# Moving operands on a fixed byte phase, forget gates without their own slab, and a shifted order of splits in a three-block transformer kernel

## The chip, the cores and the metric

One core of a Trainium2 chip runs the whole program; the other cores are idle. The metric is the device time of one execution in microseconds (us), median of the runs shown. Engines are named as in the profile: PE (TensorE matmul) with PEld (its weight loads), DVE (VectorE), ACT (ScalarE), POOL (GpSimd), SP (SyncE, which here only issues transfers).

## The reference, cut to what matters

256 tokens (272 with 16 meta tokens in front in the first layer) of width 1024 pass through three layers, all in fp32.

```python
# first_block: a = rmsnorm(h); proj = a @ w_in -> pool mixer, "forgetting" attention, stick-breaking attention
log_f = log_sigmoid(fl + forget_bias)      # fl = a @ w_in[:, 6 columns]: the forget gates, one per head
c = cumsum(log_f); s = q k^T * scale + c[q] - c[k]          # forgetting attention
h = h + concat(y_pool, y_fox, y_sb) @ w_out
h = h + (silu(rmsnorm(h) @ w_gate) * (rmsnorm(h) @ w_up)) @ w_down
# second_block, layer 0: convolution branch + block attention, h @ ab_w_out, then squared-ReLU MLP (4096 wide)
# second_block, layer 1: conv, two block-diagonal gates, linear recurrence, h @ c_w_out, then the same MLP
```

Nearly all arithmetic is in products of the 1024-wide activations with weights that are read once.

## The kernel before

**Slabs.** Every weight matrix is cut into slabs of 128 x 1024 fp32 (512 KB), 275 in all, laid out in the order of use and brought in by SP into a ring of `R` = 4 buffers `raw`. To get fp32 precision from single-pass matmuls each slab is split: ACT writes the rounded high part (`whi`, line 513), DVE subtracts to get the rest (`wlo`, line 929). Activations are split in the same way into `ahi` (ACT, lines 541, 572, 622) and `alo` (DVE, lines 947, 953), and the hidden values of the MLPs into `hidhi` and `hidlo`. A product is then three matmuls: `whi*ahi`, `whi*alo`, `wlo*ahi` (function `three`, lines 1363 to 1365).

**Columns and rows.** A slab is used in one of two forms, 24 matmuls each. As a *column* (`column`) it gives 128 output channels: the weights of chunk k meet the tokens of chunk k of `ahi`/`alo`, for k = 0 to 7, and all 24 add into one PSUM bank. As a *row* (`row`, `operand_row`, `hidden_row`) it takes one chunk of 128 inputs, so all 24 read the same chunk of tokens, and they add into 8 half banks. The MLPs alternate columns (tokens from `ahi`/`alo`) with rows (from `hidhi`/`hidlo`). The output projections OUT1, OUT2 and OUT3 are 8 rows each, row i on chunk i of `ahi`/`alo`; OUT3's first two take their chunk from `hidhi`/`hidlo` instead. Each stage begins with `first_columns`, where two columns are interleaved chunk by chunk while DVE still makes `alo`.

**Stages, with the slabs they use.** IN1 (21: one for the forget gates and 20 columns), OUT1 (8), MLP1 (66: 44 columns, 22 rows), IN2 (20 columns), OUT2 (8), MLP2 (64: 32 and 32), IN3 (16 columns), OUT3 (8), MLP3 (64). IN1's columns that also serve the meta tokens read 272 tokens from a chunk's start; all others read 256 from its 17th.

**Where the tokens lie.** A chunk of `ahi` or `alo` is 272 fp32 = 1088 bytes, that is 4 x 256 + 64. In the built program `ahi` begins at byte 82,560 of each partition and `alo` at 91,264, both 128 past a multiple of 256. Token 16 of chunk k therefore lies at byte (192 + 64 k) mod 256: 192 for k = 0 and 4, 0 for k = 1 and 5, 64 for k = 2 and 6, 128 for k = 3 and 7. `hidhi` begins at 134,720 with 1024-byte chunks, so all its chunks lie at byte 64 of 256, and so do those of `hidlo`. All weight chunks lie at byte 128.

**Forget gates.** The first slab holds the six gate columns, padded with zeros to 128. It is an ordinary column, interleaved with the first real one at the start of the program, where four *pieces* of two chunks each arrive, are split and are used one after the other. Lines 1032 to 1043 on DVE turn its result into the running sum `cum`.

**Constants.** POOL builds masks, the identity and so on from 18 us on; the semaphore `consts` counts them, and `consts_done` = 13 means all. PE waits for all 13 before the value transposes (line 1458) that follow IN1's first columns, and DVE waits for them before the scan at line 1043.

**Order.** No scheduler moves anything. The order on each engine is that of the code, by hand-written tables: `DVE_SPLITS`, `CAT2_STEP`, `RESIDUAL_ROW`, `FINAL_RESIDUAL` say in which slot `u` of the OUT2 stage DVE makes which split, `alo` and residual. `split_ahead(n)` splits slab n + 3.

## Time and profile before

| | |
|---|---|
| median of 3 runs | 887.29 us (886.36 to 1056.22) |
| profiled execution | 886.04 us |
| its span, first to last instruction | 884.3 us |
| PE busy | 868.6 us (98%), 7310 matmul records |
| PEld, DVE, ACT, POOL busy | 837.4, 607.5, 470.6, 95.0 us |
| HBM traffic | 169 GB/s over the span |
| chain that ended last | PE 87%, DVE 7%, ACT 3%, issue 1%, DMA 1% |

The span is the time between the first and the last instruction of the profiled execution; 1.7 us of the device time lie around it. A matmul's own duration in the profile overlaps its neighbours', so what a matmul costs is read from the start of one to the start of the next. An fp32 matmul has two records, one of the split kind has one.

### The profile page before, as it was taken

What the parts mean: (1) busy time and instruction counts of PE and PEld (TensorE: products, weight loads), DVE (VectorE), ACT (ScalarE), POOL (GpSimd) and SP (SyncE); (2) the same over time, 40 slices, a digit from 0 to 9 for tenths busy, and PEclk for the clock granted to TensorE, in tenths of its full rate; (3) what the DMA queues carried; (4) which work ended last, traced back from release to release, by engine and by line L of the source; (5) the groups of instructions that cost most, each with busy time, mean ns of one, the idle gap of its engine ahead of it and who ended that gap; (6) DMA issues with size and microseconds to landing.
All of it is one profiled execution on the core that took longest, in us unless ns stands there. A gap on an engine that the chain in (4) does not pass through costs nothing.

```text
span 884.3 us, 19363 instructions
## 1 busy us (share of the span) xinstructions
PE 868.6 (98%) x7310; PEld 837.4 (95%) x7310; DVE 607.5 (69%) x994; ACT 470.6 (53%) x755; POOL 95.0 (11%) x139
## 2 busy tenths in 40 slices
PE   8999999999999999999999999999999999999996
PEld 8888899999999999787999999999999999999996
DVE  4766558666566587877866666668979966666665
ACT  6556666434444385448744444445786644444443
POOL 3420002000000029611100000001110100000001
PEclk9999999999999999999999999999999999999999
DMA  7532336665655648623465555555534565555551
GB/s 250 170 118 97 118 122 223 204 191 173 204 177 181 198 147 234 175 98 125 160 225 189 183 187 187 189 188 166 166 131 158 169 214 189 189 188 185 188 174 48
DMA packets 44434, 152.10 MB, mean 172 GB/s; under 512 B 5604, under 2 KB 6884, under 8 KB 44388
## 3 DMA queue, kind: packets, MB, share of 16 engines
q1 hardware_dynamic: 41184, 145.52, 50.3%
q0 software_dynamic: 2400, 4.89, 1.8%
q10 hardware_dynamic: 804, 1.04, 0.3%
q8 instruction: 33, 0.54, 0.3%
q14 instruction: 13, 0.11, 0.0%
HBM read 148.64 MB, written 1.05 MB: 169 GB/s over the span
## 4 chain that ended last, share of the span: by engine, by line
PE 87%; DVE 7%; ACT 3%; issue 1%; DMA 1%; SPq 0%; DVEq 0%; ACTq 0%
PE bank L1363 26%; PE bank L1365 26%; PE bank L1364 26%; DVE alo L953 2%; DVE wlo L929 2%; PE bank L1713 1%; PE bank L1397 1%; PE bank L1447 1%; PE bank L1492 1%; PE bank L1469 1%; PE bank L1803 1%; ACT whi L513 1%; DMA raw<-in_slabs 1%; DVE h L963 1%; PE bank L1391 1%
## 5 line engine op out<-in xcount | busy, mean ns | idle before, releaser
L1363 PE MATMUL bank<-ahi,whi 128*128 128x256 f32 (+1 forms) x1400 | 400.4, 286 | 1.9 <-DVE alo L947 1.2
L1364 PE MATMUL bank<-alo,whi 128*128 128x256 f32 (+1 forms) x1400 | 394.0, 281 | 0.0
L1365 PE MATMUL bank<-ahi,wlo 128*128 128x256 f32 (+1 forms) x1400 | 393.9, 281 | 0.0
L929 DVE TENSOR_TENSOR wlo<-raw,whi 128x1024 fp32r<-128x1024 f32 x273 | 332.2, 1225 | 30.3 <-ACT whi L513 30.2
L513 ACT ACTIVATE whi<-raw 128x1024 fp32r<-128x1024 f32 x273 | 282.4, 1051 | 93.1 <-PE bank L1365 83.4
L1363 PEld LDWEIGHTS bank<-ahi,whi 128*128 128x128 f32 x1400 | 264.0, 189 | 6.4 <-DVE alo L947 2.6
L1364 PEld LDWEIGHTS bank<-alo,whi 128*128 128x128 f32 x1400 | 264.0, 189 | 0.4
L1365 PEld LDWEIGHTS bank<-ahi,wlo 128*128 128x128 f32 x1400 | 264.3, 189 | 0.0
L1363 PE MATMUL bank<-hidhi,whi 128*128 128x256 f32 x704 | 195.1, 277 | 0.7 <-DVE hidlo L947 0.7
L1365 PE MATMUL bank<-hidhi,wlo 128*128 128x256 f32 x704 | 195.1, 277 | 0.0
L1364 PE MATMUL bank<-hidlo,whi 128*128 128x256 f32 x704 | 194.4, 276 | 0.0
L1363 PEld LDWEIGHTS bank<-hidhi,whi 128*128 128x128 f32 x704 | 132.3, 188 | 0.9 <-DVE hidlo L947 0.9
L1364 PEld LDWEIGHTS bank<-hidlo,whi 128*128 128x128 f32 x704 | 132.2, 188 | 0.0
L1365 PEld LDWEIGHTS bank<-hidhi,wlo 128*128 128x128 f32 x704 | 132.1, 188 | 0.0
L1249 DVE SCALAR_TENSOR_TENSOR y<-bank,rstd 128x256 f32<-128x256 f32 x64 | 27.3, 426 | 119.4 <-PE bank L1365 117.4
L834 ACT ACTIVATE hidhi<-y 128x256 fp32r<-128x256 f32 x64 | 26.8, 419 | 133.1 <-DVE y L1249 130.1
L390 POOL TENSOR_TENSOR sq<-sq 128x256 f32<-128x256 f32 (+1 forms) x19 | 17.1, 912 | 320.6 <-ACT sq L545 173.9
L395 POOL TENSOR_TENSOR sq<-sq 128x256 f32<-128x256 f32 x12 | 9.9, 831 | 356.0 <-ACT sq L531 179.9
L972 DVE SCALAR_TENSOR_TENSOR proj<-bank,rstd 128x256 f32<-128x256 f32 (+1 forms) x56 | 23.7, 425 | 33.9 <-PE bank L1365 33.3
L724 ACT ACTIVATE hidhi<-y 128x256 fp32r<-128x256 f32 x22 | 9.2, 418 | 58.8 <-DVE y L1132 58.8
L953 DVE SCALAR_TENSOR_TENSOR alo<-h,par,ahi 128x256 fp32r<-128x256 f32 (+1 forms) x48 | 29.2, 672 | 0.0
L1257 DVE TENSOR_TENSOR hidlo<-y,hidhi 128x256 fp32r<-128x256 f32 x64 | 27.2, 425 | 2.3
(223 smaller groups left out, 724.4 us busy)
## 6 DMA issues: line engine op xcount, KB each, us to landing
raw<-in_slabs SPq DMA_DIRECT2D x273, 512.0 KB, 3.5
shared<-in_convw POOLq DMA_DIRECT2D x4, 512.0 KB, 6.8
shared<-zpad POOLq DMA_DIRECT2D x48, 35.5 KB, 3.6
raw<-in_slabs SPq DMA_DIRECT2D x8, 128.0 KB, 5.4
vtok<-in_gatew POOLq DMA_DIRECT2D x2, 512.0 KB, 5.4
out<-y SPq DMA_DIRECT2D x4, 256.0 KB, 2.8
h<-in_xT ACTq DMA_DIRECT2D x3, 272.0 KB, 5.2
h<-in_xT SPq DMA_DIRECT2D x1, 272.0 KB, 3.5
```

Of the source, the lines that this page charges most:

```text
L390: pool.tensor_tensor(a, a, sq[:, 2 * j + 1, lo:], ALU.add).then_inc(sum_ready, 1)
L395: ins = pool.tensor_tensor(sq[:, a, NMETA:], sq[:, a, NMETA:], sq[:, b, NMETA:], ALU.add)
L513: act.activation(whi[:, n % R, :, :], raw[:, n % R, :, :], ACT.Copy).then_inc(hi_done, 1)
L834: act.activation(hidhi[:, hid_buf(f, FF2 - 1), :], hid[:, f % 2, :], ACT.Square).then_inc(hid_hi, 1)
L929: dve.tensor_tensor(wlo[:, n % R, :, :], raw[:, n % R, :, :], whi[:, n % R, :, :].bitcast(F32), ALU.subtract).then_inc(lo_done, 1)
L953: dve.scalar_tensor_tensor(alo[:, k, lo:], h[:, k, lo:], par[:, g:g + 1], ahi[:, k, lo:].bitcast(F32), ALU.mult, ALU.subtract).then_inc(al ...
L972: dve.scalar_tensor_tensor(proj[:, d, lo:], src[:, lo:T1], scale, rstd[:, lo:], ALU.mult, ALU.mult).then_inc(gemm_evac, 1)
L1249: dve.scalar_tensor_tensor(hid[:, f % 2, :], col_bank(f)[:, NMETA:T1], 0.0, rstd[:, NMETA:], ALU.max, ALU.mult).then_inc(gemm_evac, 1)
L1257: dve.tensor_tensor(hidlo[:, b, :], hid2[:, f % 2, :], hidhi[:, b, :].bitcast(F32), ALU.subtract).then_inc(hid_lo, 1)
L1363: pe.matmul(dst, hi, xh, start=start, stop=False, skip_group_check=True)
L1364: pe.matmul(dst, hi, xl, start=False, stop=False, skip_group_check=True)
L1365: return pe.matmul(dst, lo, xh, start=False, stop=stop, skip_group_check=True)
```

## The change

1. **Layout.** `ahi` and `alo` get chunks of `STRIDE_A` = 320 fp32 (1280 bytes, 5 x 256), with a pad of 128 bytes ahead, so that in the built program they begin at 82,688 and 92,928, both multiples of 256. Token 16 of every chunk is at byte 64 of 256; token 0, where IN1's wide columns begin, is at byte 0. A second pad keeps `hidhi`/`hidlo` at byte 64. Weights stay at byte 128.
2. **Forget gates.** Their slab goes (274 slabs are left). DVE multiplies the 6 x 8 gate columns with the norm gain into a small zeroed buffer `flg`; PE multiplies them in plain fp32 with the raw x, in 8 matmuls of 32 columns that go to four column groups of one bank (`forget_parts`); DVE copies the result, and one more fp32 matmul with a 0/1 matrix `fl_sel`, made by POOL, adds the four groups.
3. **Start.** The two columns that are interleaved are now both real, and each piece's `alo` matmuls follow its `ahi` matmuls (`first_pieces`). The warm-up is 10 matmuls, then the first two gate matmuls, then 5. DVE adds two of POOL's pair sums (`quad_sum`), so that the statistics of the first norm take 2 fp32 matmuls and not 4, and stand in the middle of a column.
4. **OUT2.** The second of two splits of slot 14 goes to slot 15; the residuals of slot 18 go to the end; `ahi` and `alo` of chunk 5 come in slot 18; the layer norm's Exp moves one slot behind its Ln on ACT.
5. **OUT3.** Gated output 1, `ahi` and `alo` of chunk 1 and one split come one step earlier.

```diff
+STRIDE_A, PAD_A = 320, 32
-WARM_UP = 16
+WARM_UP, WARM_UP_2 = 10, 5
-OUT1 = IN1 + 21
+OUT1 = IN1 + 20
-CAT2_STEP = {12: 0, 13: 1, 15: 2, 16: 3, 17: 4}
+CAT2_STEP = {12: 0, 13: 1, 15: 2, 16: 3, 17: 4, 18: 5}
-FINAL_RESIDUAL, RESIDUAL_ROW = {18: (0, 1)}, {5: (2, 3), 6: (4, 5), 7: (6, 7)}
-DVE_SPLITS = {13: (-1,), 14: (0, 1), 16: (2,), 17: (3,), 18: (4,)}
+RESIDUAL_ROW = {5: (0, 1, 2), 6: (3, 4, 5), 7: (6, 7)}
+DVE_SPLITS = {13: (-1,), 14: (0,), 15: (1,), 16: (2,), 17: (3,), 18: (4,)}
-        ahi = sb("ahi", [P, KC, T1], F32R)
-        alo = sb("alo", [P, KC, T1], F32R)
+        sb("pad_a", [P, PAD_A])
+        ahi = sb("ahi", [P, KC, STRIDE_A], F32R)
+        alo = sb("alo", [P, KC, STRIDE_A], F32R)
...
+        sb("pad_hid", [P, PAD_A])
...
+            dve.wait_ge(fl_zero, 1)
+            f0, g0 = COL["forget"], COL["norm1"]
+            dve.tensor_tensor(flg[:, :, 0:FOX_HEADS], par[:, f0:f0 + FOX_HEADS * KC].rearrange("p (k m) -> p k m", k=KC),
+                              par[:, g0:g0 + KC].rearrange("p (k m) -> p k m", m=1).broadcast_to((P, KC, FOX_HEADS)),
+                              ALU.mult).then_inc(fl_w, 1)
...
             split(2)
-            split_early(IN1)
+            dve.wait_ge(fl_parts, 1)
+            dve.tensor_scalar(fl_part, acc_bank[1][:, 0:T1], 1.0, None, ALU.mult).then_inc(fl_copied, 1)
+            quad_sum(0)
+            split(3)
+            quad_sum(1)
+            split(4)
...
+            def forget_parts(ks):
+                for k in ks:
+                    pe.wait_ge(x_loaded[k // 2], 16)
+                    c = FL_M * (k % 4)
+                    ins = pe.matmul(acc_bank[1][c:c + FL_M, 0:T1], flg[:, k, :], h[:, k, :], start=(k < 4), stop=(k >= 4),
+                                    skip_group_check=True)
...
+            def first_pieces():
+                for i in range(PIECES):
...
+                    for k in (2 * i, 2 * i + 1):
+                        first_high(IN1, A_NORM1, k, 0)
+                    if i == 0:
+                        forget_parts((2, 3))
+                    if i == PIECES - 1:
+                        forget_parts((4, 5, 6, 7))
+                    for k in (2 * i, 2 * i + 1):
+                        first_low(IN1, A_NORM1, k, 0)
...
-            first_columns(IN1, A_NORM1, 0)
+            warm_up(WARM_UP)
+            pe.wait_ge(fl_w, 1)
+            forget_parts((0, 1))
+            warm_up(WARM_UP_2)
+            first_pieces()
...
-                if i == 15:
+                if i == 14:
                     gated_output(1)
+                if i == 14:
+                    operand_lo(A_LRU, 1)
+                    split_ahead(IN3 + i)
```

DVE at the start of the program, behind the four pieces, up to the scan that makes `cum`; before (L929 is a split, L972 takes a column's result, L1032 and L1034 the gates, L1041 and L1043 the running sum):

```order
L929 TENSOR_TENSOR wlo<-raw,whi 128x1024 x2
L1032 TENSOR_TENSOR shared<-bank,rstd 70x272
L1034 TENSOR_SCALAR shared<-shared,fbias 70x272
L972 SCALAR_TENSOR_TENSOR proj<-bank,rstd 128x272
L929 TENSOR_TENSOR wlo<-raw,whi 128x1024
...
L1041 SCALAR_TENSOR_TENSOR shared<-shared 70x272
L1043 SCALAR_TENSOR_TENSOR cum<-shared 70x272
```

The same place in the changed kernel (L955 is a split, L998 takes a column, L1064 copies the gates' parts, L1061 is `quad_sum`, L1082 the scan):

```order
L955 TENSOR_TENSOR wlo<-raw,whi 128x1024
L1064 TENSOR_SCALAR prob<-bank 128x272
L1061 TENSOR_TENSOR sq<-sq 128x272
L955 TENSOR_TENSOR wlo<-raw,whi 128x1024
L1061 TENSOR_TENSOR sq<-sq 128x272
L955 TENSOR_TENSOR wlo<-raw,whi 128x1024
L998 SCALAR_TENSOR_TENSOR proj<-bank,rstd 128x272
L1076 TENSOR_TENSOR shared<-bank,rstd 70x272
L1077 TENSOR_SCALAR shared<-shared,fbias 70x272
...
L1080 SCALAR_TENSOR_TENSOR shared<-shared 70x272
L1082 SCALAR_TENSOR_TENSOR cum<-shared 70x272
```

Three splits now stand ahead of the first column's result where two stood, and the first column is taken ahead of the gates.

DVE in slots 14 to 18 of OUT2; before (L988 closes slot 14's scores, L994 and L997 normalise in slot 15, L947 is an `alo`, L1225 the convolution branch's product, L1166 a residual):

```order
L988 TENSOR_REDUCE nmax<-ssb 128x1 x2
L929 TENSOR_TENSOR wlo<-raw,whi 128x1024 x2
L994 RECIPROCAL rinv<-rsum 128x2
L997 TENSOR_SCALAR prob<-prob,rinv 128x256 x2
L947 TENSOR_TENSOR alo<-af,ahi 128x256
L1225 SCALAR_TENSOR_TENSOR af<-sq,af 128x256 x2
...
L1166 SCALAR_TENSOR_TENSOR h<-h,par,r 128x256 x2
L947 TENSOR_TENSOR alo<-af,ahi 128x256 x3
L929 TENSOR_TENSOR wlo<-raw,whi 128x1024
```

The same place in the changed kernel (L1014, L955, L1020, L1023, L973, L1265 and L1205 are the same operations):

```order
L1014 TENSOR_REDUCE nmax<-ssb 128x1 x2
L955 TENSOR_TENSOR wlo<-raw,whi 128x1024
L1020 RECIPROCAL rinv<-rsum 128x2
L1023 TENSOR_SCALAR prob<-prob,rinv 128x256 x2
L973 TENSOR_TENSOR alo<-af,ahi 128x256
L955 TENSOR_TENSOR wlo<-raw,whi 128x1024
L1265 SCALAR_TENSOR_TENSOR af<-sq,af 128x256 x2
...
L973 TENSOR_TENSOR alo<-af,ahi 128x256 x2
L955 TENSOR_TENSOR wlo<-raw,whi 128x1024
L1205 SCALAR_TENSOR_TENSOR h<-h,par,r 128x256 x3
```

One split has moved from ahead of the normalisation to behind it and an `alo`, and no residual stands ahead of the last `alo` operands any more.

## Rows read from the trace of the kernel before

**Rows 1.** The page: the chain that ended last, by engine.

```profile
PE 87%; DVE 7%; ACT 3%; issue 1%; DMA 1%; SPq 0%; DVEq 0%; ACTq 0%
```

**Rows 2.** PE timeline, MLP1; start and duration in us, engine, line, operation; slab beginnings.

```profile
162.01 0.28 PE L1363 MATMUL bank<-ahi,whi 128*128 128x256 f32 x1
...
164.85 0.28 PE L1363 MATMUL bank<-hidhi,whi 128*128 128x256 f32 x1
...
167.59 0.28 PE L1363 MATMUL bank<-ahi,whi 128*128 128x256 f32 x1
...
316.41 0.28 PE L1363 MATMUL bank<-hidhi,whi 128*128 128x256 f32 x1
...
319.13 0.28 PE L1363 MATMUL bank<-hidhi,whi 128*128 128x256 f32 x1
```

**Rows 3.** PE timeline, rows 4 to 7 of OUT1: third and twenty-third matmul of each.

```profile
122.80 0.28 PE L1365 MATMUL bank<-ahi,wlo 128*128 128x256 f32 x1
...
125.16 0.28 PE L1364 MATMUL bank<-alo,whi 128*128 128x256 f32 x1
...
126.06 0.28 PE L1365 MATMUL bank<-ahi,wlo 128*128 128x256 f32 x1
...
128.44 0.28 PE L1364 MATMUL bank<-alo,whi 128*128 128x256 f32 x1
...
128.91 0.28 PE L1365 MATMUL bank<-ahi,wlo 128*128 128x256 f32 x1
...
131.18 0.28 PE L1364 MATMUL bank<-alo,whi 128*128 128x256 f32 x1
...
131.99 0.28 PE L1365 MATMUL bank<-ahi,wlo 128*128 128x256 f32 x1
...
134.37 0.28 PE L1364 MATMUL bank<-alo,whi 128*128 128x256 f32 x1
```

**Rows 4.** Timelines of POOL, DVE and PE, 22 to 38 us.

```profile
22.65 4.68 POOL L382 TENSOR_SCALAR_AFFINE_SELECT shared<-shared 128x128 f32<-128x128 f32 x1
...
32.63 0.20 POOL L436 MEMSET zpad<- 128x120 f32 x1
...
32.94 0.72 DVE L1043 TENSOR_TENSOR_SCAN cum<-shared 70x272 f32<-70x272 f32 x1
...
36.13 0.82 PE L1458 MATMUL bank<-ident,proj 128*128 128x128 f32 x6
...
37.80 0.17 DVE L1051 TENSOR_SCALAR cumT<-bank 128x12 f32<-128x12 f32 x1
```

**Rows 5.** IN2: POOL and PE timelines, and line 465 by itself.

```profile
341.96 7.89 POOL L465 DMA_DIRECT2D shared<-zpad  x16 [0.29 <-POOL zpad L458]
...
DMA to landing us min/median/max: 1.9/3.6/6.1
...
355.98 1.93 PE L1713 MATMUL bank<-shared 128*32 128x256 f32 x32
```

**Rows 6.** OUT2: DVE and PE timelines, 412 to 425 us; in brackets idle before.

```profile
412.09 1.23 DVE L929 TENSOR_TENSOR wlo<-raw,whi 128x1024 fp32r<-128x1024 f32 x1 [0.66 <-ACT whi L513]
...
414.10 0.66 PE L1483 MATMUL bank<-ident,prob 128*128 128x128 f32 x4 [1.67 <-DVE prob L997]
...
423.47 0.87 DVE L1166 SCALAR_TENSOR_TENSOR h<-h,par,r 128x256 f32<-128x256 f32 x2
...
424.74 0.39 PE L1363 MATMUL bank<-ahi,whi 128*128 128x256 f32 x1 [0.77 <-DVE alo L947]
```

**Rows 7.** Windows of IN3 and OUT3: length, then busy PE, PEld, DVE, ACT, POOL.

```profile
622.00:651.50 29.50, 29.50 (x226) 28.70 (x225) 27.50 (x44) 22.01 (x40) 4.62 (x6) 1.00 0.53 179
...
672.50:690.50 18.00, 17.91 (x144) 17.16 (x144) 17.59 (x32) 9.31 (x14) 0.00 (x0) 1.00 0.52 175
```

**Rows 8.** PE groups by line and form: busy us, mean ns of one.

```profile
L1447 PE MATMUL bank<-sq,ones 128*128 128x272 f32 x8 | 2.0, 392 | 0.0
L1500 PE MATMUL bank<-ones 128*128 128x128 f32 x32 | 6.7, 406 | 1.1 <-POOL eps L410 1.1
```

More of the change, by code:

```diff
@@ L79 @@
 EARLY = tuple(n + i for n in (IN1, MLP1, IN2, MLP2, IN3, MLP3) for i in range(2)) + (IN2 - 1, IN3 - 1)
-EARLY_LO = tuple(n + i for n in (MLP1, IN2, MLP2, IN3, MLP3) for i in (-1, 0)) + (IN1,)
+EARLY_LO = tuple(n + i for n in (MLP1, IN2, MLP2, IN3, MLP3) for i in (-1, 0)) + (IN1, IN1 + 1)
 QF, KF, VF, PU, QS, KS, VS = 0, 3, 6, 9, 11, 14, 17
@@ L410, in _ @@
             pool.memset(eps2[:, :], EPS * EPS).then_inc(consts, 1)
+            pool.memset(flg, 0.0).then_inc(fl_zero, 1)
+            step(pool.memset(fl_sel, 0.0))
+            for i in range(-2, 4):
+                ins = pool.affine_select(out=fl_sel, in_=fl_sel, compare_op=ALU.not_equal, fill=1.0, base=-FL_M * i,
+                                         pattern=[[-1, FL_P]], channel_multiplier=1)
+                if i < 3:
+                    step(ins)
+            ins.then_inc(fl_ones, 1)
             pair_sums(N_NORM1, 0)
@@ L633, in _ @@
             norm_factor(N_NORM1, stat_bank[:, 0:T1], 0)
-            for n in range(IN1, IN1 + FOX_READY + 1):
+            for n in range(IN1, IN1 + FOX_READY):
                 split_ahead(n)
@@ L768, in _ @@
                         transposed(u // 2 - 1, FOX_S, moba_copies)
+                    if u == LN_VAR_STEP + 1:
+                        act.wait_ge(ln_log, 1)
+                        act.activation(ln_r[:, :], std[:, NMETA:], ACT.Exp, scale=-0.5).then_inc(ln_std, 1)
                     if u in PAIR_STEP:
@@ L1235, in _ @@
                 operand_lo(A_CAT2, i)
-            for i in range(max(CAT2_STEP.values()) + 1, KC):
+            for i in range(max(OUT2_STEP.values()) + 1, KC):
                 split_ahead(OUT2 + i)
@@ L1306, in _ @@
             for i, c in enumerate(IN3_ORDER):
-                if i == 15:
+                if i == 14:
                     gated_output(1)
-                take(IN3 + i, col_bank(i), c, ahead=IN3 + i < OUT3 - 1 and i != 10)
+                take(IN3 + i, col_bank(i), c, ahead=IN3 + i < OUT3 - 1 and i not in (10, 14))
+                if i == 14:
+                    operand_lo(A_LRU, 1)
+                    split_ahead(IN3 + i)
                 if i == 13:
@@ L1368, in slab_ready, with column @@
                 pe.wait_ge(lo_done, n + 1 + R * q)
-            def column(n, bank, q=0, lo=NMETA):
+            def column(n, bank, q=0, lo=NMETA, amid=None):
                 slab_ready(n, q)
                 for k in range(KC):
-                    ins = three(bank[:, lo:T1], n, k, ahi[:, k, lo:], alo[:, k, lo:], k == 0, k == KC - 1)
+                    if amid and k == 3:
+                        amid()
+                    ins = three(bank[:, lo:T1], n, k, ahi[:, k, lo:T1], alo[:, k, lo:T1], k == 0, k == KC - 1)
@@ L1375, in column @@
                 ins.then_inc(slab_used, 1)
-            def first_columns(n, s, lo=NMETA):
-                if n > IN1:
-                    slab_ready(n + 1)
-                for k in range(KC):
-                    if n == IN1 and k % 2 == 0:
-                        if k < KC - 2:
-                            pe.wait_ge(piece_lo, k + 2)
-                        else:
-                            slab_ready(n + 1)
-                    pe.wait_ge(ahi_ready, KC * s + k + 1)
-                    for b in range(2):
-                        dst, slot = gemm_bank[b][:, lo:T1], (n + b) % R
-                        for w in (whi, wlo):
-                            pe.matmul(dst, w[:, slot, k, :], ahi[:, k, lo:], start=(k == 0 and w is whi), stop=False,
-                                      skip_group_check=True)
-                for k in range(KC):
-                    pe.wait_ge(alo_ready, KC * s + k + 1)
-                    for b in range(2):
-                        dst, slot = gemm_bank[b][:, lo:T1], (n + b) % R
-                        ins = pe.matmul(dst, whi[:, slot, k, :], alo[:, k, lo:], start=False, stop=(k == KC - 1),
-                                        skip_group_check=True)
-                        if k == KC - 1:
-                            ins.then_inc(slab_used, 1)
@@ new lines, in first_high, with first_low @@
+            def first_high(n, s, k, lo=NMETA):
+                pe.wait_ge(ahi_ready, KC * s + k + 1)
+                for b in range(2):
+                    dst, slot = gemm_bank[b][:, lo:T1], (n + b) % R
+                    for w in (whi, wlo):
+                        pe.matmul(dst, w[:, slot, k, :], ahi[:, k, lo:T1], start=(k == 0 and w is whi), stop=False,
+                                  skip_group_check=True)
+            def first_low(n, s, k, lo=NMETA):
+                pe.wait_ge(alo_ready, KC * s + k + 1)
+                for b in range(2):
+                    dst, slot = gemm_bank[b][:, lo:T1], (n + b) % R
+                    ins = pe.matmul(dst, whi[:, slot, k, :], alo[:, k, lo:T1], start=False, stop=(k == KC - 1),
+                                    skip_group_check=True)
+                    if k == KC - 1:
+                        ins.then_inc(slab_used, 1)
@@ L1448, in stats, with first_stats @@
                 ins.then_inc(stat_ready, 1)
+            def first_stats():
+                for j in range(2):
+                    pe.wait_ge(quad_ready, j + 1)
+                    ins = pe.matmul(stat_bank[:, 0:T1], ones[:, :], sq[:, 4 * j, :], start=(j == 0), stop=(j == 1))
+                ins.then_inc(stat_ready, 1)
             def plain_stats():
```

115 lines of the change are left out of this document (67 added, 48 removed).

## The prediction, made before the changed kernel was run

> **What bounds the kernel now.** I read the page's chain first: PE is 87% of it [rows 1], so time is won by making PE's stream shorter, or by removing the few places where it waits. Then the PE timeline by slab, from the start of one slab's 24 matmuls to the next. In MLP1 a column takes 164.85 - 162.01 = 2.84 us and the hidden row behind it 167.59 - 164.85 = 2.74 us; a hidden row behind another takes 319.13 - 316.41 = 2.72 us [rows 2]. Both have the same weights, the same 256 tokens, no wait. That is 118.3 ns a matmul against 113.3.
>
> Rows of OUT1 tell what differs. In each, 20 matmuls lie between the third and the twenty-third: row 4 (tokens at byte 192 of 256) takes (125.16 - 122.80)/20 = 118 ns, row 5 (byte 0) 119, row 6 (byte 64) 113.5, row 7 (byte 128) 119.3 [rows 3]. Tile, shape and neighbours are the same; only the chunk, and so the byte phase, changes. Hidden rows lie at byte 64 too and have the same short pace. So the phase sets the pace, and a column, which visits each phase twice, has nearly the mean of the four, (118 + 119 + 113.5 + 119.3)/4 = 117.5, against 118.3 measured.
>
> **Part 1, layout.** *MLP columns.* Beyond the two in `first_columns`, MLP1 has 42 columns and MLP2 and MLP3 30 each: 102, all fed back to back. At byte 64 everywhere a column costs 2.72 us (a row behind a row) to 2.74 (a row behind a column), so it saves 0.10 to 0.12. Only one thing in the trace makes 2.74 of 2.72: the entry from a tile at another phase, and that goes; I take 0.115. 102 x 0.115 = 11.7 (10.2 to 12.2). *Hidden rows behind columns*, some 80, may lose that entry too: 0 to 0.02 each, I take 0.016: 1.3 (0 to 1.7).
>
> *IN2*, 18 more columns on PE's path: 18 x 0.115 = 2.1. But the first convolution group at 355.98 needs POOL's 16 small transfers, the last issued at 341.96 + 7.89 = 349.85 with up to 6.1 us from issue to landing [rows 5]: it may land at 355.4 or so, 0.5 us ahead of its use. Nine columns stand ahead of it and would bring PE there 1.0 us sooner. Half a microsecond turns into a wait: 1.5 (0.5 to 2.0).
>
> *IN3.* Eight columns run there beside gates, and each would save 0.11. DVE is busy 27.50 of 29.50 us in that window [rows 7] and feeds the gates, and behind them ACT's chain of table loads leads to OUT3. I take 0.3 (0 to 0.9). *OUT3.* DVE is busy 17.59 of 18.00 us [rows 7]: its rows go at DVE's pace, and shorter matmuls give nothing.
>
> *The rest.* OUT1's rows would save 0.7 (six rows of eight, 24 x 4.5 to 6 ns each), but the chain there runs through ACT and DVE between some of them: 0.5 (0.2 to 0.7). The interleaved first columns of three stages, 48 matmuls x 5 ns where DVE doesn't gate them: 0.3. In IN1 five columns of 256 gain 0.1 each, and the 15 of 272 tokens go from mixed phases to byte 0: (119 - 117.5) x 272/256 x 24 = 0.04 us more each, 0.6 in all at worst, and next to nothing against the 118.3 that columns have. Net 0.1 (-0.3 to 0.3).
>
> Layout together: 11.7 + 1.3 + 1.5 + 0.3 + 0.5 + 0.3 + 0.1 = 15.7.
>
> The Trainium skill ("SBUF — State Buffer", section "Operand start alignment") gives only legality for a start address (a multiple of the element size) and says that its runs timed nothing; in the section "Door 1: The DMA port swizzle" of the same page it names 16-byte lines as the grain at which access gets slow. All four phases are multiples of 16, so by that rule the layout is worth nothing; the rows above disagree, and they decide.
>
> **Parts 2 and 3, the start.** What goes: one slab, 24 x 118.3 x 272/256 ns = 3.0 us of PE, its split, 512 KB; two of four fp32 matmuls of the statistics, 2.0/4 = 0.5 us each [rows 8], so 1.0. What comes: 8 narrow fp32 matmuls. The convolution's groups have this form (32 columns, four column groups): 32 records, four groups of four, in 1.93 us [rows 5], 0.48 us for four at once. In three batches (2, 2 and 4) that is 1.4, and 0.5 for the sum over groups. DVE gets a copy and two sums, each less than its 272-wide scan's 0.72 us [rows 4], and loses a split. Each piece's `alo` matmuls fall partly into gaps that PE has between pieces, about 1 us. PE would so be through its first seven real columns near 31 us, 5 us before 36.13 [rows 4].
>
> What is late next is POOL. Its last constant ends at 32.63 + 0.20 = 32.8, only just ahead of DVE's scan at 32.94 [rows 4]. The change leaves that chain where it is. PE waits for it at the transposes (now 36.13), and DVE waits for it at the scan with two column results and two splits queued behind. After the scan comes one column's result, which the transposes need: 32.94 + 0.72 + 0.4 = 34.1 instead of 36.13 (the 0.4 is a guess under the scan's 0.72). The softmax chain behind `cumT` at 37.80 [rows 4] gains less, about 1.1, since the queued result and splits stand ahead of it; it has slack behind. I take 2.1. Bounds: 0.5, if the attention chain sets the pace at first; 5.0, if POOL's step of 4.68 us at 22.65 [rows 4] is an accident and takes a fraction of that next time: the constants are then ready before PE.
>
> **Part 4, OUT2.** At 414.10 PE has waited 1.67 us for the normalisation, which stood behind the split that DVE began at 412.09 [rows 6]. DVE was free from 412.09 - 0.66 = 411.43. With that split behind it the normalisation can go then, and PE 1.6 us sooner. The moved split is for slab OUT2+4, used two rows after the one that follows here: two rows of PE work cover it, and if they didn't, 1.2 us would be back. At 424.74 PE has waited 0.77 us for the `alo` of row 5, behind two residuals (0.87 us at 423.47) [rows 6]; with these moved and `alo` 5 in slot 18 the wait goes. Rows here save 0.7 in pace. But all DVE work remains and the two residuals now stand in the tail, ahead of the additions that open MLP2. Following DVE step by step with the trace's durations, that point comes 2.4 us sooner (0.8 to 3.1), pace of the rows included. ACT's Exp one slot later lets the transposed probabilities through first and delays DVE's layer norm by about its own length, ahead of a wait of DVE for PE's scores: nothing, and at most 0.5 if that wait is gone.
>
> **Part 5, OUT3.** PE's row 1 comes sooner, row 2 does not, since DVE does the same work in another order: 0 (-0.3 to 0.4).
>
> **Sum.** 15.7 + 2.1 + 2.4 = 20.2 us, from 886.0 to 865.8 for the profiled execution. The median of before lies 1.2 us above its profiled execution and the lowest run 0.3: I add 0.7, **866.5 us**. Ends added up: savings of 12 to 25, so 862 to 875 with all terms at one end at once.
>
> **Rivals.** (a) *Columns don't follow.* Within a column at 162 us the two chunks at byte 64 don't stand out as row 6 does; the pace is smeared. If columns are held at 118 ns by something else (all 24 add into one bank), the layout only helps rows: 20.2 - 11.7 - 1.3 - 1.5 - 0.3 = 5.4 saved, 881. Against it: the mean of the phases meets the column's pace within 1 ns. (b) *The phase is no cause at all*, and row 6 and the hidden rows are fast by some neighbour on another engine: start and OUT2 alone, 2.1 + 2.4 = 4.5 saved, 882. Against it: three equal tiles with three paces [rows 3], which no neighbour explains. This is what the Trainium skill's page quoted above would give. (c) *New waits.* The start gives 0.5, IN2 another 0.5, OUT2 0.8 as its tail takes back what the stall gave, and the hidden rows nothing: 20.2 - 1.6 - 1.0 - 1.6 - 1.3 = 14.7 saved; with the columns at 0.10 another 1.5 less: 871.5 to 873. (d) *Slower than before:* PE's clock. The warm-up's 32 records of 128 columns take 6.7 us, the statistics' 8 of 272 columns 2.0 [rows 8]: 1.6 ns a column against 0.9, so PE starts near its lower level (1.2 GHz) and is at the upper (2.4) later, after the warm-up. The warm-up now has a wait for DVE and narrow matmuls in it. If full pace came later, each microsecond of full-pace work done at half pace costs one more; beyond 20 us of such work, that is if half pace lasted through the whole of IN1's first columns, the kernel is slower. With some 24 us of such work between the first piece and the transposes: 866.5 + 24 = 890.
>
> **Chances.** Forecast 0.82 (own range 861 to 871), (a) 0.08, (b) 0.03, (c) 0.05, (d) 0.02. The range takes in the forecast's, and a part of (c): 861 to 872. Two per cent, 17.7 us, is what a measurement of this kernel tells from no change; the line is at 869.5. Faster by more: 0.82 x 0.93 = 0.76. Slower by more: 0.01. Within: 0.23.
>
> **What would show it.** MLP columns at 2.72 to 2.74 us, and rows of OUT1 all at 113.5 ns a matmul (layout); 2.84 means (a), rows still apart (b). PE's value transposes near 34 us with DVE's scan starting right after POOL's last constant (start). No wait of PE for the normalisation in slot 16 of OUT2, and the additions that open MLP2 about 2.4 us sooner than the columns alone explain. OUT3's period still 3.0 us a row. I would be wrong by most if columns kept their pace.

## The result, and the profile after

The changed kernel takes **882.93 us** in the median of ten runs (876.51 to 884.41), the kernel before 886.31 (885.76 to 1056.22). Over all runs the ratio of the two is 0.9937, 95% interval 0.9911 to 0.9964: 0.6% faster, less than the 2% that I set as the line. (The medians alone give 0.9962, since six of the ten runs lie in the upper of the two groups below.) Ratios leave out two disturbed runs, one of the kernel before at 1056.22 us and one of e7 at 2982.77 us. The forecast was 866.5, with a range from 861 to 872. It was wrong, by 16 us.

The ten times are not spread evenly. Four lie at 876.5 to 876.9 and six at 882.8 to 884.4, with nothing between, while the kernel before lies within 2 us but for one run. The mean granted clock is 0.998 or 0.999 in all ten. That the time has two values will turn out to be the core of the case.

The page's chain, by engine, answers to [rows 1] and hardly differs. PE is still the bound:

```profile
PE 87%; DVE 6%; ACT 3%; issue 1%; DMA 1%; POOL 1%; SPq 0%; DVEq 0%; ACTq 0%; POOLq 0%
```

The profiled execution is one of the slower group (884.41 us, span 882.7). The PE timeline of MLP1, slab beginnings, answers to [rows 2]; a column, a hidden row, a column, a column:

```profile
157.89 0.28 PE L1405 MATMUL bank<-ahi,whi 128*128 128x256 f32 x1
...
160.72 0.28 PE L1405 MATMUL bank<-hidhi,whi 128*128 128x256 f32 x1
...
163.55 0.28 PE L1405 MATMUL bank<-ahi,whi 128*128 128x256 f32 x1
...
166.37 0.28 PE L1405 MATMUL bank<-ahi,whi 128*128 128x256 f32 x1
```

Every slab takes 2.83 us. The columns gained 0.01 of the 0.115 us foreseen, and the hidden rows, which had 2.72 to 2.74 before at the same byte phase, lost 0.09 to 0.11. So it is in all three MLPs. The view by windows shows it in one row each (length, then busy time and number of records of PE, PEld, DVE, ACT and POOL, granted clock of PE, DMA share, GB/s); the windows lie inside MLP1, MLP2 and MLP3:

```profile
160.00:300.00 140.00, 140.00 (x1191) 140.00 (x1190) 85.43 (x116) 61.41 (x84) 0.00 (x0) 1.00 0.60 186
450.00:600.00 150.00, 150.00 (x1276) 150.00 (x1276) 90.59 (x133) 63.98 (x79) 0.00 (x0) 1.00 0.56 188
...
705.00:845.00 140.00, 140.00 (x1191) 140.00 (x1190) 85.92 (x124) 61.30 (x76) 0.00 (x0) 1.00 0.58 189
```

Window over number of matmuls is nearly the pace: 140/1191, 150/1276 and 140/1191 give 117.5 ns three times. The count takes in the two or three matmuls that a window's edges cut, so this reads 0.2 to 0.3 ns low; slab by slab the two paces are 117.8 ns (2.83 us a slab) and 113.3 ns (2.72 us). A window of only short-paced matmuls would hold 140/0.1133 = 1236 or 150/0.1133 = 1324. The granted clock is 1.00 of its upper level (2.4 GHz) in all three, so this is not the clock.

But the short pace is still there, in the same layout. Rows 4 and 5 of OUT1, both now at byte 64, third and twenty-third matmul of each, answer to [rows 3]:

```profile
118.73 0.28 PE L1407 MATMUL bank<-ahi,wlo 128*128 128x256 f32 x1
...
121.01 0.28 PE L1406 MATMUL bank<-alo,whi 128*128 128x256 f32 x1
...
121.91 0.28 PE L1407 MATMUL bank<-ahi,wlo 128*128 128x256 f32 x1
...
124.26 0.28 PE L1406 MATMUL bank<-alo,whi 128*128 128x256 f32 x1
```

(121.01 - 118.73)/20 is 114 ns, (124.26 - 121.91)/20 is 117.5. Tiles of the same phase and shape, in neighbouring rows, have two paces.

The start went better than forecast. POOL, DVE and PE timelines, answering to [rows 4]:

```profile
23.39 0.29 POOL L395 TENSOR_SCALAR_AFFINE_SELECT shared<-shared 128x128 f32<-128x128 f32 x1
...
28.53 0.20 POOL L458 MEMSET zpad<- 128x120 f32 x1
...
29.89 0.72 DVE L1082 TENSOR_TENSOR_SCAN cum<-shared 70x272 f32<-70x272 f32 x1
...
32.29 0.82 PE L1537 MATMUL bank<-ident,proj 128*128 128x128 f32 x6
```

The transposes begin 3.84 us sooner (forecast: 2.1), with POOL done well ahead. In OUT2 the wait of 1.67 us [rows 6] is gone: the transposes of `prob` follow with no idle time, and the split stands behind (PE and DVE timelines):

```profile
408.75 0.66 PE L1562 MATMUL bank<-ident,prob 128*128 128x128 f32 x4
...
409.14 1.22 DVE L955 TENSOR_TENSOR wlo<-raw,whi 128x1024 fp32r<-128x1024 f32 x1
```

Where the time went can be added up from the PE timeline. I take the start of each stage's first columns, after minus before: MLP1 130.40 - 134.61 = -4.2 us; IN2 319.01 - 321.85 = -2.8; MLP2 427.09 - 433.31 = -6.2; IN3 610.71 - 614.17 = -3.5; MLP3 690.28 - 693.78 = -3.5; the span's end 882.7 - 884.3 = -1.6. The start won 4.2, IN2 and OUT2 together 3.4, and the three MLPs gave back 1.4, 2.8 and 1.9.

### The profile page after: what moved, and what is told of

Same layout as the page of the kernel before. It is cut to its first block, busy times and chain, and to the rows that moved or that the text cites. A ratio compares the mean times of both kernels' runs of the same rounds, so it can differ in the third digit from the quotient of the medians.

```text
span 882.7 us, 19329 instructions
## 1 busy us (share of the span) xinstructions
PE 870.2 (99%) x7298; PEld 837.3 (95%) x7298; DVE 607.3 (69%) x997; ACT 469.2 (53%) x754; POOL 91.7 (10%) x147
## 4 chain that ended last, share of the span: by engine, by line
PE 87%; DVE 6%; ACT 3%; issue 1%; DMA 1%; POOL 1%; SPq 0%; DVEq 0%; ACTq 0%; POOLq 0%
PE bank L1405 26%; PE bank L1407 26%; PE bank L1406 26%; DVE alo L979 2%; PE bank L1799 1%; DVE wlo L955 1%; PE bank L1435 1%; PE bank L1571 1%; DVE h L989 1%; PE bank L1548 1%; PE bank L1427 1%; PE bank L1889 1%; PE bank L1519 1%; DMA raw<-in_slabs 1%; ACT whi L535 1%
## 5 line engine op out<-in xcount | busy, mean ns | idle before, releaser
L955 DVE TENSOR_TENSOR wlo<-raw,whi 128x1024 fp32r<-128x1024 f32 x272 | 331.0, 1225 | 26.6 <-ACT whi L535 26.6
L1407 PEld LDWEIGHTS bank<-ahi,wlo 128*128 128x128 f32 x1392 | 261.5, 188 | 0.0
L1405 PE MATMUL bank<-hidhi,whi 128*128 128x256 f32 x704 | 197.8, 281 | 0.6 <-DVE wlo L955 0.6
L1406 PE MATMUL bank<-hidlo,whi 128*128 128x256 f32 x704 | 197.7, 281 | 0.0
L1407 PE MATMUL bank<-hidhi,wlo 128*128 128x256 f32 x704 | 197.7, 281 | 0.0
L1406 PEld LDWEIGHTS bank<-hidlo,whi 128*128 128x128 f32 x704 | 134.0, 190 | 0.0
L998 DVE SCALAR_TENSOR_TENSOR proj<-bank,rstd 128x256 f32<-128x256 f32 (+1 forms) x56 | 23.5, 424 | 33.0 <-PE bank L1407 30.2
```

The source lines that it names most:

```text
L955: dve.tensor_tensor(wlo[:, n % R, :, :], raw[:, n % R, :, :], whi[:, n % R, :, :].bitcast(F32), ALU.subtract).then_inc(lo_done, 1)
L998: dve.scalar_tensor_tensor(proj[:, d, lo:], src[:, lo:T1], scale, rstd[:, lo:], ALU.mult, ALU.mult).then_inc(gemm_evac, 1)
L1405: pe.matmul(dst, hi, xh, start=start, stop=False, skip_group_check=True)
L1406: pe.matmul(dst, hi, xl, start=False, stop=False, skip_group_check=True)
L1407: return pe.matmul(dst, lo, xh, start=False, stop=stop, skip_group_check=True)
```

## The experiments

Three theories went into the first runs. **1:** tiles at one shared phase have two paces, and an unbroken stream keeps the one that it is in. **2:** the new address of the hidden operands within 512 bytes is slow. **3:** the layout is harmless and the other parts did it. **4** came with the later runs: the pace is drawn at a stage's entry and nothing in the stage moves it.

### e1_layout: the kernel before with the layout alone

```diff
+STRIDE_A, PAD_A = 320, 32
...
-        ahi = sb("ahi", [P, KC, T1], F32R)
-        alo = sb("alo", [P, KC, T1], F32R)
+        sb("pad_a", [P, PAD_A])
+        ahi = sb("ahi", [P, KC, STRIDE_A], F32R)
+        alo = sb("alo", [P, KC, STRIDE_A], F32R)
...
+        sb("pad_hid", [P, PAD_A])
...
```

> The kernel before with the new layout alone (chunks of 1280 bytes, tokens at byte 64 of 256, the hidden operands 3328 bytes higher). Theory 1, one shared phase: where every tile that PE reads has the same byte phase, the stream of matmuls keeps whatever pace it is in, 117.8 or 113.3 ns, and nothing in the MLP moves it out; columns and hidden rows then both take 2.83 us in the MLP, a column gains 0.01 and a hidden row loses 0.09. With 102 columns and 84 hidden rows that is about 5 to 6 us slower than before: 890 to 892. Theory 2, place: the new address of the hidden operands (320 of 512 bytes, formerly 64 of 512) is what slowed the hidden rows, and a column whose chunks alternate between 64 and 320 of 512 is slow for the same reason; it expects the same sum here, 890 to 892, with the same slabs at 2.83. Rival 3, the layout is harmless and the loss of the changed kernel comes from its other parts (the order of the work, which engines are busy beside the MLP): then hidden rows stay at 2.72 to 2.74 and the time is 874 (columns at 2.73) to 886 (columns at 2.84).

Ten runs: 870.5, 870.8, 872.4, 877.0, 877.1, 877.2, 883.7, 883.7, 883.9 and 890.7 us. These are four groups, some 6.5 to 7 us apart, round a median of 877.2; the kernel before, run beside it, has 885.9. The mean granted clock is 0.997 to 0.999 in all ten. The profile is of the run at 876.95. Its windows:

```profile
160.00:300.00 140.00, 140.00 (x1238) 140.00 (x1237) 88.91 (x121) 62.74 (x86) 0.00 (x0) 1.00 0.60 194
450.00:600.00 150.00, 150.00 (x1325) 150.00 (x1325) 96.22 (x140) 67.13 (x83) 0.00 (x0) 1.00 0.57 193
705.00:845.00 140.00, 140.00 (x1191) 140.00 (x1190) 85.01 (x124) 60.48 (x75) 0.00 (x0) 1.00 0.55 187
```

MLP1 and MLP2 run at the short pace, columns and rows alike (2.72 us a slab), and MLP3 at the long one (2.83), in one execution of one program. My number for this run was wrong (890 to 892 came up once in ten), but theory 1's mechanism stands there to be read. Theory 2 is out: MLP1's hidden rows are at their new address and short. So is theory 3: the layout alone does it.

The price fits. An MLP holds 62 to 64 slabs behind its first columns, 24 matmuls each: 63 x 24 x (117.8 - 113.3) ns = 6.8 us for one stage at the long pace. So I read the groups as none, one, two and three stages at the long pace. Profiles show three of the four: one long stage here at 877, two in e4 at 877, three in the changed kernel at 884 (the last two kernels have the other parts of the change as well, worth 7.4 us by e2). The fourth, no long stage, was profiled only in kernels with an added step (e5, e10, e11). With none the layout saves 885.9 - 870.5 = 15.4 us, and I had written 15.7.

The long pace has a mark of its own in the weight loads (PEld). In e1, MLP3 in two groups of instructions, then MLP2 in one:

```profile
L1369 PEld LDWEIGHTS bank<-ahi,wlo 128*128 128x128 f32 x200 | 38.4, 192 | 0.0
L1367 PEld LDWEIGHTS bank<-ahi,whi 128*128 128x128 f32 x199 | 37.4, 188 | 0.0
...
L1369 PEld LDWEIGHTS bank<-ahi,wlo 128*128 128x128 f32 x220 | 41.3, 188 | 0.0
```

Of the three loads of a product, one takes 192 ns at the long pace and the other two 188. It is so in all nine long MLPs in the profiles of the changed kernel, e1, e3 and e4, and which of the three it is differs from stage to stage; in their three short MLPs all take 188. So the long pace is a rhythm of three that the stream holds. What starts it is not shown.

The PE timeline of the same run shows a switch, where MLP1's first hidden row follows its second column:

```profile
144.38 0.28 PE L1367 MATMUL bank<-ahi,whi 128*128 128x256 f32 x1
...
146.98 0.28 PE L1368 MATMUL bank<-alo,whi 128*128 128x256 f32 x1
147.09 0.28 PE L1369 MATMUL bank<-ahi,wlo 128*128 128x256 f32 x1
147.21 0.28 PE L1367 MATMUL bank<-hidhi,whi 128*128 128x256 f32 x1
...
149.94 0.28 PE L1367 MATMUL bank<-ahi,whi 128*128 128x256 f32 x1
...
152.66 0.28 PE L1367 MATMUL bank<-ahi,whi 128*128 128x256 f32 x1
```

147.21 - 144.38 = 2.83 for the column; then 2.73 for the row and 2.72 for the next column, and so to the end of MLP1. There is no gap and no step of phase, so an unbroken stream can change its pace. Of the twelve MLPs in the four profiles with this layout and no step (the changed kernel, e1, e3, e4), MLP1 of e1 and of e4 do it, both here; the other ten hold one pace from the first slab behind the first columns to the last. In the changed kernel's profile the same passage from column to row switches nothing.

### e2_order: the changed kernel with the old layout

```diff
-STRIDE_A, PAD_A = 320, 32
+STRIDE_A = T1
...
-        sb("pad_a", [P, PAD_A])
...
-        sb("pad_hid", [P, PAD_A])
```

> The changed kernel with the old layout: chunks of 1088 bytes, no padding; all other parts stay. Theories 1 and 2: hidden rows are back at 2.72 to 2.74 us and columns at 2.84; the start's gain of 4.2 us and OUT2's of 2.6 remain, so 886.3 - 6.8 = 879.5 (878.5 to 880.5). Rival 3 (the other parts slow the hidden rows): hidden rows stay at 2.83 and the time is 884 or more.

878.54 us (878.42 to 878.87), ratio 0.9912 [0.9895, 0.9929]: four runs within half a microsecond, one group. All other parts together are worth 885.9 - 878.5 = 7.4 us; the forecast had 2.1 + 2.4 less 0.7 for the rows' pace. Hidden rows are short again, columns long. So in the changed kernel the layout costs 4.4 us in the median (882.9 against 878.5): it saves 1.8 in the lower group and costs 5 in the upper.

### e3_again: the changed kernel once more

> The changed kernel once more, to have a second profile of it. Its ten times lie in two groups, four at 876.5 to 876.9 and six at 882.8 to 884.4. Theory 1: the profile of an execution of the lower group has hidden rows, or all slabs, of a part of the MLP stages at 2.72 us; one at 884 looks as the first profile did, with 2.83 everywhere. Theory 2 has no reason for two groups, since the addresses are the same in each: it expects each profile to show 2.83 in the hidden rows, and the two groups then come from somewhere else.

877.5 us median of six, again two groups: 876.5 to 877.9 four times and 883.0 to 883.2 twice. The profile fell on one at 883.15 and is as the first, 1191, 1276 and 1191 matmuls in the three windows. By e1's arithmetic the lower group has one MLP at the short pace; no profile fell on it here, but the next experiment shows that pattern.

### e4_hid: the hidden operands at byte 64 of 512

```diff
-        sb("pad_hid", [P, PAD_A])
+        sb("pad_hid", [P, PAD_A + 64])
```

> The changed kernel with 256 bytes more ahead of the hidden operands: they lie at byte 64 of 512 again, as in the kernel before, and the columns stay as they are. Theory 2 (place within 512 bytes): hidden rows return to 2.72 to 2.74 us, some 84 x 0.09 = 7.6 us less than 884, so 876 to 877, in every run. Theory 1 (one shared phase of 256): nothing changes, the time is that of the changed kernel, 876.5 to 884.4 in two groups, and hidden rows are not tied to 2.73.

877.3 us (876.7 to 877.6), four runs. By its number this is theory 2's forecast (876 to 877). The windows say otherwise:

```profile
160.00:300.00 140.00, 140.00 (x1238) 140.00 (x1237) 89.03 (x121) 63.63 (x87) 0.00 (x0) 1.00 0.60 194
450.00:600.00 150.00, 150.00 (x1276) 150.00 (x1275) 93.27 (x135) 64.61 (x80) 0.00 (x0) 1.00 0.55 186
705.00:845.00 140.00, 140.00 (x1191) 140.00 (x1190) 85.00 (x123) 60.06 (x75) 0.00 (x0) 1.00 0.56 187
```

MLP1 is short throughout, its columns too, which weren't moved; MLP2 and MLP3 are long throughout, their hidden rows too, which were. The address does not make rows short. It is one stage out of three, the count that I read into the changed kernel's lower group. Whether the address shifts the odds is open: all four runs here are in that group, against eight of sixteen of the changed kernel. A time that meets a forecast does not show its mechanism; the counts per stage do.

### e5_kick: the last chunk at another phase

In the kernel before, a hidden row behind a column of mixed phases always found the short pace. So I brought one step of phase back into each column:

```diff
+def at(k, lo, hi):
+    o = 16 if k == KC - 1 else 0
+    return slice(o + lo, o + hi)
...
-                    ins = three(bank[:, lo:T1], n, k, ahi[:, k, lo:T1], alo[:, k, lo:T1], k == 0, k == KC - 1)
+                    ins = three(bank[:, lo:T1], n, k, ahi[:, k, at(k, lo, T1)], alo[:, k, at(k, lo, T1)], k == 0, k == KC - 1)
...
```

All other places that write or read `ahi` and `alo` follow suit.

> The changed kernel, but the last of the eight chunks of both operands lies 64 bytes further (its tokens at byte 128 of 256, the other seven at byte 64), so that each column ends on another phase. In the runs so far an unbroken stream of tiles at one phase kept the pace it came in with for a whole MLP stage, 113.3 or 117.8 ns, while in the kernel before every hidden row behind a column of mixed phases fell to 113.3 within five matmuls. Theory 1a, the step to another phase resets the stream: columns and rows of all three MLP stages run at 113.3 except for a few matmuls around the step, a column 2.72 to 2.78 us; 884 less 186 slabs x 0.11, plus 92 steps x 0.03, is 866 to 868, and in one group. Theory 1b, the stream falls into the short pace only when a run of tiles of one phase follows mixed ones, and three matmuls of another phase undo it: columns 2.80 to 2.84, rows 2.72, 877 to 880. Theory 4, the pace is drawn at the stage's entry and nothing in the stage moves it: 863.5, 870.3, 877 or 884, in groups.

**865.26 us** (864.99 to 865.72), ratio 0.9764 [0.9748, 0.9781], one group: theory 1a. It is 21.0 us faster than before (886.3 beside it) and 17.7 faster than the changed kernel, for 64 bytes. Theory 4, in which nothing inside a stage moves the pace, is out. The windows:

```profile
160.00:300.00 140.00, 140.00 (x1231) 140.00 (x1231) 88.55 (x120) 63.03 (x87) 0.00 (x0) 1.00 0.61 193
450.00:600.00 150.00, 150.00 (x1321) 150.00 (x1321) 97.92 (x151) 68.70 (x90) 1.75 (x3) 1.00 0.58 192
705.00:845.00 140.00, 140.00 (x1233) 140.00 (x1233) 87.86 (x128) 62.26 (x78) 0.00 (x0) 1.00 0.57 187
```

113.5 to 113.7 ns in all three, as windows count. The PE timeline where a column's last chunk (byte 128) is followed by a hidden row (byte 64):

```profile
158.68 0.28 PE L1413 MATMUL bank<-ahi,wlo 128*128 128x256 f32 x1
158.79 0.28 PE L1411 MATMUL bank<-ahi,whi 128*128 128x256 f32 x1
158.91 0.27 PE L1412 MATMUL bank<-alo,whi 128*128 128x256 f32 x1
159.03 0.28 PE L1413 MATMUL bank<-ahi,wlo 128*128 128x256 f32 x1
159.14 0.28 PE L1411 MATMUL bank<-hidhi,whi 128*128 128x256 f32 x1
159.26 0.28 PE L1412 MATMUL bank<-hidlo,whi 128*128 128x256 f32 x1
159.38 0.28 PE L1413 MATMUL bank<-hidhi,wlo 128*128 128x256 f32 x1
159.50 0.28 PE L1411 MATMUL bank<-hidhi,whi 128*128 128x256 f32 x1
159.61 0.28 PE L1412 MATMUL bank<-hidlo,whi 128*128 128x256 f32 x1
```

The eight distances take 159.61 - 158.68 = 0.93 us, 116 ns each against 113.3: the matmuls around the step take a little more, then the short pace is back. Such a column takes 2.73 to 2.74 us; I estimate that all steps together cost about 2 us, against 863 for the layout at the short pace throughout (878.5 - 15.4, from e2 and e1).

### e6_hid128 and e7_byte0: is byte 64 special?

Both start from the changed kernel. e6 puts the hidden operands at byte 128 and leaves the columns at 64:

```diff
-        sb("pad_hid", [P, PAD_A])
+        sb("pad_hid", [P, PAD_A + 16])
```

e7 puts the tokens of every operand at byte 0:

```diff
-STRIDE_A, PAD_A = 320, 32
+STRIDE_A, PAD_A = 320, 16
...
-        sb("pad_hid", [P, PAD_A])
+        sb("pad_hid", [P, PAD_A + 16])
```

> The changed kernel with the hidden operands at byte 128 of 256, the columns all at byte 64. Theory 1a (a step between phases resets the stream): columns behind a row, rows behind a column fall to 113.3 in all stages, 866 to 868. The reading of the prediction, that byte 64 itself is the short phase: columns 2.72, hidden rows 119.5 ns x 24 = 2.87 us, 84 x 0.15 = 12.6 us above 863.5, so 876. Theory 4 (drawn at the entry): groups 6.8 us apart, as in the changed kernel.

877.5 us (876.8 to 878.0), one group. MLP2 by groups of instructions (busy us, mean ns of one; the overlapping duration is 276 or 277 at the short pace and 280 or more at others):

```profile
L1405 PE MATMUL bank<-hidhi,whi 128*128 128x256 f32 x213 | 60.1, 282 | 0.0
L1405 PE MATMUL bank<-ahi,whi 128*128 128x256 f32 x216 | 59.9, 277 | 0.0
```

Columns at byte 64 are short in all three stages (2.72 to 2.74 us), rows at byte 128 take 2.86, and 2.88 behind another row. Both ideas of the expectation hold at once: the step from 128 back to 64 resets the stream, and byte 128 itself is slow.

> The changed kernel with every operand's tokens at byte 0 of 256 in place of 64. If byte 64 is the short phase, as the prediction read the rows of OUT1 (byte 0 took 119 ns, byte 64 took 113.5), each of the 186 slabs of the MLP stages takes 2.86 us in every execution: 884 + 186 x 0.03 = 889 or more, in one group. If what counts is only that all tiles share a phase (theories 1 and 4), the same two paces as with byte 64 come back, in groups between 863.5 and 884.

890.2 us, ratio 1.004 [1.0024, 1.0056]; the MLP1 window has 1183 matmuls, and MLP2 and MLP3 are alike (1266 and 1183). A slab takes 2.85 us, 118.7 ns a matmul, and none of this kernel's MLPs has a short one. Sharing a phase is not enough.

### e8_before_hid0: hidden operands of the kernel before at byte 0

```diff
+        sb("pad_hid", [P, 48])
```

> The kernel before with its hidden operands at byte 0 of 256 in place of 64, nothing else. Its columns still mix four phases, so each row's stream starts anew. If byte 64 is the short phase: hidden rows take 119 ns x 24 = 2.86 us, 84 x 0.13 = 11 us more than before, 897. If a run of one phase, whichever it is, falls to the short pace: hidden rows stay at 2.72 to 2.74 and the time at 886.

894.64 us, ratio 1.0095 [1.0079, 1.0112]. The same group of hidden rows in MLP2, whose mean was 277 at byte 64:

```profile
L1364 PE MATMUL bank<-hidhi,whi 128*128 128x256 f32 x214 | 60.2, 281 | 0.0
```

Rows cost 2.84 to 2.85 us (one 2.89), and the kernel 894.6 - 886.3 = 8.3 us more. Of the phases tried, byte 64 is the one with a short pace; the prediction's reading of [rows 3] was right so far.

### e9_out2: OUT2's order alone

```diff
-CAT2_STEP = {12: 0, 13: 1, 15: 2, 16: 3, 17: 4}
+CAT2_STEP = {12: 0, 13: 1, 15: 2, 16: 3, 17: 4, 18: 5}
...
-FINAL_RESIDUAL, RESIDUAL_ROW = {18: (0, 1)}, {5: (2, 3), 6: (4, 5), 7: (6, 7)}
-
-DVE_SPLITS = {13: (-1,), 14: (0, 1), 16: (2,), 17: (3,), 18: (4,)}
+RESIDUAL_ROW = {5: (0, 1, 2), 6: (3, 4, 5), 7: (6, 7)}
+
+DVE_SPLITS = {13: (-1,), 14: (0,), 15: (1,), 16: (2,), 17: (3,), 18: (4,)}
...
```

> The kernel before with the changes of OUT2 alone (splits and residuals of DVE, ACT's Exp one slot later, the sixth operand row in slot 18). The prediction's term is 2.4 us, its bounds 0.8 and 3.1, 0.7 of it from the pace of rows, which isn't changed here: 886.0 - 1.7 = 884.3. The trace of the changed kernel with the old layout has this stretch 2.5 us shorter: 883.5. If the gain is really that of the start, which let the later stage run on other terms, this kernel is at 886.

883.67 us (883.46 to 884.37), ratio 0.9975 [0.9965, 0.9985]: 2.2 us, with no help from the start and none from the pace. The remaining 7.4 - 2.2 = 5.2 us are the start and OUT3.

This run, with the old layout, also limits what a step of phase does. Row 6 of OUT2 lies at byte 64 and follows row 5, at byte 0, without a gap. Its third and twenty-third matmul (PE timeline):

```profile
425.18 0.28 PE L1367 MATMUL bank<-ahi,wlo 128*128 128x256 f32 x1
...
427.53 0.28 PE L1366 MATMUL bank<-alo,whi 128*128 128x256 f32 x1
```

(427.53 - 425.18)/20 is 117.5 ns: the long pace behind a step, as in the same row of e2. Row 6 of OUT1 in the kernel before, at the same phases, took the short one [rows 3].

### e10_layout_kick: layout and step, without the other parts

> The kernel before with the layout, and the last chunk of both operands at byte 128 of 256 as in the run that kept every MLP stage at the short pace. If the step of phase is what holds the pace, the layout gives here what it gave there, without the other parts: 865.3 + 7.7 (the other parts, measured without the layout) = 873.0, in one group. If the other parts were needed for it (the order of work around a stage's entry draws the pace), groups 6.8 us apart as for the layout alone, 870.5 to 890.7.

872.69 us (871.88 to 874.02), ratio 0.9856 [0.9839, 0.9872], one group, 0.3 from the sum, and all three MLPs short in the profile (columns and rows 2.72 to 2.74 us). The step works by itself, and the parts add up.

### e11_kick0 and e12_kick_one: which step, how long

Both start from the changed kernel. e11 is e5 with the last chunk at byte 0 of 256:

```diff
+    o = 48 if k == KC - 1 else 0
```

e12 is e5 with only the low operand's last chunk at byte 128:

```diff
-                    ins = three(bank[:, lo:T1], n, k, ahi[:, k, lo:T1], alo[:, k, lo:T1], k == 0, k == KC - 1)
+                    ins = three(bank[:, lo:T1], n, k, ahi[:, k, lo:T1], alo[:, k, at(k, lo, T1)], k == 0, k == KC - 1)
```

> The changed kernel with its last chunk at byte 0 of 256 instead of 128 or 64. If any step to another phase resets the stream to the short pace: one group at 865 to 866, as with byte 128. If the step from byte 128 to 64 has something of its own: groups 6.8 us apart between 863.5 and 884, or the long pace everywhere, 884.

869.5 us (869.0 to 869.7), one group: in the MLPs byte 0 resets the stream too, but costs more. The MLP1 window has 1222 matmuls instead of 1231, and a hidden row behind a column takes 2.75 us.

> The changed kernel with only the low operand's last chunk at byte 128: one matmul of the 24 of a column is at another phase instead of three. If one matmul is enough to reset the stream: one group, and up to 92 columns x 2 x 0.005 = 1 us less than with three, 864.3 to 865.3. If it takes more of them: groups, 863.5 to 884, or columns at a pace between.

871.8, 867.6, 866.1, 866.2 and 866.8 us. The profile is of the 871.8:

```profile
160.00:300.00 140.00, 140.00 (x1229) 140.00 (x1229) 88.66 (x120) 62.68 (x86) 0.00 (x0) 1.00 0.61 192
450.00:600.00 150.00, 150.00 (x1276) 150.00 (x1275) 92.15 (x135) 64.60 (x81) 0.00 (x0) 1.00 0.58 186
705.00:845.00 140.00, 140.00 (x1232) 140.00 (x1231) 87.84 (x127) 61.97 (x76) 0.00 (x0) 1.00 0.60 193
```

MLP2 kept the long pace throughout, with a step of one matmul in each of its columns: one in 24 does not always reset the stream. It isn't cheaper either: 866.1 at best against 865.0.

## Why the prediction was wrong, and where it was right

**The step that failed** is in part 1: "At byte 64 everywhere a column costs 2.72 us (a row behind a row) to 2.74 (a row behind a column)", and with it 102 x 0.115 = 11.7, the 1.3 for hidden rows and the 1.5 for IN2. The rows were read rightly: byte 64 allows the short pace, other phases don't (e7, e8, and e6's rows). But every short run of tiles in [rows 2, 3] had come to byte 64 from another phase. I took what I saw behind a step of phase for a property of the phase. At byte 64 there are two paces, 113.3 and 117.8 ns, and the layout removed the very steps that had led to the short one in the rows that I read. Without them a stream takes one pace or the other behind an interruption and then mostly keeps it for a whole MLP. I had even noted the entry from another phase, as a cost that would go (0.115 rather than 0.10, and the 1.3); it was what the short pace hung on in the MLPs. In the rows of OUT2 a step was not enough (e9, e2).

The sizes were right for the case I assumed. In e1's profile MLP1, up to IN2's first columns, is 187.24 - 182.00 = 5.2 us shorter than before (foreseen 42 x 0.115 + 20 x 0.016 = 5.2) and MLP2 180.86 - 176.88 = 4.0 (foreseen 3.9); with all MLPs short the layout alone saves 15.4 us against 15.7. IN2's 1.5 was too much: its stage is 0.8 us shorter in e5 and 0.4 in e1. That the 865.3 of e5 lies by the forecast's 866.5 is in part luck: the other parts gave 7.4 us where I had 3.8 without the rows' pace, and the steps took 2 back. The changed kernel has three of its three MLPs at the long pace in both of its profiles, and by the distance of the groups two of them in its lower group, 6.8 us each. The range failed because I set it by the sizes of terms and gave the mechanism 0.82.

Two slips of arithmetic don't bear on this. The rows shown for row 7 give (134.37 - 131.99)/20 = 119.0 ns and not 119.3. The high ends of all terms add up to 26.6 and not 25, so "all terms at one end" begins at 860.

**Rivals.** (a), columns held at 118 ns, gave 881, close to 882.9, and is not the cause: columns do run at 2.72 us in e1 and e4 and at 2.73 to 2.74 in e5, and hidden rows lost as well, which (a) excluded. That its number came near is chance. It had noticed the right oddity, that in a column the chunks at byte 64 don't stand out. (b), no effect of the phase, is refuted: moving only the hidden operands by 192 bytes costs 8.3 us (e8); its 882 came near the result for another reason. The Trainium skill, "SBUF — State Buffer", in its section "Operand start alignment" states legality only and has nothing that tells bytes 0, 64 and 128 apart in speed; the traces do, with 2.72 to 2.74 us for a hidden row at byte 64 before and 2.84 to 2.85 at byte 0 (e8). (c), new waits, is not what the profile shows: the waits of OUT2 are gone and the loss lies in MLPs where PE is busy throughout. (d), a late clock, didn't come either: in the changed kernel 24 matmuls of 272 tokens take 3.14 us from 10.20 us on, as they do later (3.12 from 38.89).

**The start** was mis-sized: 2.1 forecast, 4.2 at MLP1's entry, 4.6 in e2. PE's own path was well worked out ("near 31 us": 32.3 after, 31.3 in e5). What failed is "What is late next is POOL". Its step of 4.68 us was the accident that the upper bound named. It took 1.42 us in e1, where the start is that of the kernel before, and there POOL was done by 29.5 and the transposes still began at 35.78 (POOL and PE timelines of e1):

```profile
22.64 1.42 POOL L386 TENSOR_SCALAR_AFFINE_SELECT shared<-shared 128x128 f32<-128x128 f32 x1
...
29.31 0.20 POOL L440 MEMSET zpad<- 128x120 f32 x1
...
35.78 0.82 PE L1462 MATMUL bank<-ident,proj 128*128 128x128 f32 x6
```

So POOL's constants bound next to nothing even before: ready 3.3 us sooner, they brought the transposes 0.35 us. The start had been PE's. In e2 and e5 DVE's scan does wait 1.41 us for POOL's last constant, but PE reaches the transposes at 31.55 and 31.29 us without a gap.

**OUT2**: 2.4 forecast, 2.2 measured alone (e9), of which I had put 0.7 on the pace of rows; without that, 1.7 forecast. The steps of the reasoning hold: the waits of 1.67 and 0.77 us are gone. **OUT3**: its period is still 3.0 us a row in the changed kernel (rows begin at 675.07 and 678.07), as I had written.

## What to carry to other kernels

When a trace shows a fast case, ask what came right ahead of each instance before making it the only case: removing the variety may remove what led to it. Look at all times of a kernel and not at the median alone; groups at equal distances point to a state with a price, and counting instructions in a fixed window of each stage shows which stage was in it. Of the layouts run here the best has the tokens at byte 64 of 256 and three matmuls of each column at byte 128 (e5, 865.3 us).
